# Hybrid decoder step on one core: GpSimd multiplies the prompt attention's probabilities by gate over sum

## The reference, cut to what matters

```
def masked_softmax(s, mask):
    m = jnp.max(jnp.where(mask, s, NEG_INF), axis=-1, keepdims=True)
    e = jnp.exp(jnp.where(mask, s - m, NEG_INF))
    return e / jnp.maximum(jnp.sum(e, axis=-1, keepdims=True), 1e-30)

o = g[:, :, 0] * o_c + g[:, :, 1] * o_s + g[:, :, 2] * o_w
```

## Time and profile before

| | before |
|---|---|
| median of three runs | 1538.82 us |
| the profiled execution, its own time | 1537.42 us |
| its span in the profile | 1535.6 us |
| PE busy | 94% |
| VectorE busy | 36% |
| ScalarE busy | 30% |
| GpSimd busy | 7% |
| the attention stage (871.2 to 1025.9 us) | 154.7 us |

### The profile page before, as it was taken

How to read it: one execution, slowest core, us unless ns; L and a number is a source line. 1 busy time by engine, 2 the same in 40 slices (tenths; PEclk the granted TensorE clock), 3 DMA queues, 4 the chain that set the end, 5 groups by cost and what they waited for, 6 DMA issues and landing times.

```text
span 1535.6 us, 28068 instructions
## 1 busy us (share of the span) xinstructions
PE 1438.0 (94%) x11334; PEld 1324.6 (86%) x11334; DVE 555.3 (36%) x1151; ACT 464.1 (30%) x751; POOL 112.9 (7%) x122
## 2 busy tenths in 40 slices
PE   7997999999999996999998989889789999999996
PEld 5676999999999996999998835459789999999995
DVE  0106323332323225335323274745443233232324
ACT  0115333332311114122212346643253333332111
POOL 0402000000001112000000000004320000000110
PEclk9998999999999997999999869989889999999998
DMA  9893444444433232232284323313212322323321
GB/s 347 291 369 110 139 162 137 163 137 161 133 92 87 84 103 54 86 93 69 83 97 157 126 81 102 99 50 116 83 56 82 95 83 86 92 65 87 86 84 67
DMA packets 83541, 180.21 MB, mean 117 GB/s; under 512 B 18341, under 2 KB 43429, under 8 KB 81742
## 3 DMA queue, kind: packets, MB, share of 16 engines
q1 hardware_dynamic: 83470, 179.23, 37.6%
HBM read 173.07 MB, written 10.28 MB: 119 GB/s over the span
## 4 chain that ended last, share of the span: by engine, by line
PE 86%; ACT 4%; DVE 4%; DMA 2%; SPq 2%; issue 2%; ACTq 0%; DVEq 0%
PE PS L1411 71%; PE PS L1334 4%; PE PS L1432 2%; DMA raw<-in_w_in 2%; PE PS L1603 1%; PE PS L1615 1%; SPq L574 1%; DVE rinv L937 1%; PE PS L1438 1%; PE PS L1315 1%; ACT uh L704 1%; PE PS L1348 1%; SPq L562 1%; PE PS L1628 1%; ACT sp L815 1%
## 5 line engine op out<-in xcount | busy, mean ns | idle before, releaser
L1411 PE MATMUL PS<-uh,wh 128*128 128x272 f32 x2032 | 428.8, 292 | 34.9 <-DVE ul L955 26.9
L930 DVE TENSOR_TENSOR wl<-raw,wh 128x1024 fp32r<-128x1024 f32 (+2 forms) x215 | 239.8, 1116 | 587.4 <-ACT wh L679 587.1
L679 ACT ACTIVATE wh<-raw 128x1024 fp32r<-128x1024 f32 (+2 forms) x215 | 203.6, 948 | 816.6 <-PE PS L1411 803.1
L1411 PE MATMUL PS<-uh,wl 128*128 128x272 f32 x2032 | 422.3, 290 | 0.0
L1411 PE MATMUL PS<-ul,wh 128*128 128x272 f32 x2032 | 421.7, 289 | 0.0
L1411 PEld LDWEIGHTS PS<-uh,wh 128*128 128x128 f32 x2032 | 320.5, 190 | 38.9 <-issue 36.1
L1411 PEld LDWEIGHTS PS<-ul,wh 128*128 128x128 f32 x2032 | 321.8, 190 | 0.0
L1411 PEld LDWEIGHTS PS<-uh,wl 128*128 128x128 f32 x2032 | 320.2, 190 | 0.0
L1411 PE MATMUL PS<-hh,wh 128*128 128x272 f32 x704 | 145.7, 288 | 0.9 <-DVE tmp L1004 0.9
L1411 PE MATMUL PS<-hh,wl 128*128 128x272 f32 x704 | 145.7, 288 | 0.0
L1411 PE MATMUL PS<-hl,wh 128*128 128x272 f32 x704 | 145.1, 288 | 0.0
(11 more groups left out here) (221 smaller groups left out, 1244.5 us busy)
## 6 DMA issues: line engine op xcount, KB each, us to landing
raw<-in_w_gu SPq DMA_DIRECT2D x88, 512.0 KB, 3.6
ada_t<-in_w_ada_t SPq DMA_DIRECT2D x44, 512.0 KB, 4.4
raw<-in_w_in SPq DMA_DIRECT2D x39, 512.0 KB, 3.6
ada<-in_w_ada SPq DMA_DIRECT2D x7, 2048.0 KB, 9.7
raw<-in_w_dn SPq DMA_DIRECT2D x32, 384.0 KB, 3.1
raw<-in_w_dn SPq DMA_DIRECT2D x32, 320.0 KB, 2.9
ch<-in_cmp_pages SPq DMA_DIRECT2D x64, 128.0 KB, 4.1
kv<-in_sel_pages SPq DMA_DIRECT2D x128, 64.0 KB, 1.9
```

The source lines that it names most:

```text
L679: e.activation(wh[:, u % SPLITS, 0:n, :], raw[:, u % RAWS, 0:n, :], ACT.Copy).then_inc(hi_ready, 1)
L930: e.tensor_tensor(wl[:, u % SPLITS, 0:n, :], raw[:, u % RAWS, 0:n, :], f(wh[:, u % SPLITS, 0:n, :]), ALU.subtract).then_inc(lo_ready, 1)
L1411: ins = mm(o[:, a, :], w[:, u % SPLITS, k, :], x[:, k0 + k, HT * a:HT * a + HT], start=(first and k == 0 and w is wh and x is xh), stop=(l ...
```

## The change

VectorE no longer multiplies the probabilities. After the factor is made it copies the four factors of the job from slot 5 to slot 0 of `stp` (the negative maximum there has been used by then) and raises a new semaphore, `p_factor`. GpSimd has a new function, `p_weights`, called for the 24 jobs in order between its part of the second norm and the addition of the mixers. It waits for the factor of the job and does the four multiplications in place. It raises the same semaphore, `p_prob`, on which the transposes wait as before.

```diff
+        p_factor = sem("p_factor")
...
+            def p_weights(j):
+
+                i, br, _ = JOBS[j]
+                n = nkeys(i, br)
+                e.wait_ge(p_factor, j + 1)
+                for r in range(GQ):
+                    e.tensor_scalar(sp[j % 3][:, r, 0:n], sp[j % 3][:, r, 0:n], stp[:, j % 3, 0, r:r + 1], None,
+                                    ALU.mult).then_inc(p_prob, 1)
+
             for n in range(4):
                 if n == 2:
+                    for j in range(len(JOBS)):
+                        p_weights(j)
                     for m in range(KD):
...
                 if br == 0 and i == 0:
                     chain(e.tensor_scalar(s[:, 5, :], s[:, 5, :], cst[:, C_VAL:C_VAL + 1], None, ALU.mult))
-                for r in range(GQ):
-                    e.tensor_scalar(sp[j % 3][:, r, 0:n], sp[j % 3][:, r, 0:n], s[:, 5, r:r + 1], None,
-                                    ALU.mult).then_inc(p_prob, 1)
+                e.tensor_copy(s[:, 0, :], s[:, 5, :]).then_inc(p_factor, 1)
```

## The result

The changed kernel takes 1578.78 us, median of four runs (1576.74 to 1580.95), against 1538.68 for the kernel before in the same comparison. The ratio is 1.0261, interval 1.0243 to 1.0279: 40 us slower (37 to 43). Forecast were 1551 us and a range to 1564, so the direction was right and the size was not. The profiled execution has a span of 1576.5 us, 40.9 more than before.

The account below looks back on a forecast made before the run. The order of work in the attention stage, not a full engine, was taken as the bound. Latency 7.7, contention 1.5 and clock 3.0 us make 12.2 on 1537.4: 1549.6, forecast 1551 against the median, range 1543 to 1564.

Parts of the forecast that it names:

- What bounds the kernel: Attention stage: no engine is full, the order of work bounds it; the multiplication's latency counts, VectorE mostly has time to spare.
- the price of GpSimd's multiplication: GpSimd's multiplication of one head: 0.24 us at 32 columns plus 1.0 ns a column, 0.72 us for 512 keys.
- bound from above: Upper limit for GpSimd's multiplication, from its sum of two tensors: 2.18 ns a column, 1.29 us for 512.
- the dear rival: GpSimd multiplies at line 618's price: latencies 18.0 us, with job 14, contention and clock 27, so 1566; chance 0.16.
- the sum's 12.2 us: Whole forecast loss: 7.7 us of added latency, 1.5 of GpSimd and VectorE delaying each other, 3.0 of lower PE clock.
- room: Time from the end of a job's fourth multiplication to when PE could use it; nearly 3 us in job 8.
- the ring: Last jobs: turn, copy, next job's exponentials, factor, multiplication, turn; jobs 21 to 23 add 3 x 1.02 us.
- looked the same: Jobs 2, 3, 5, 6, 9, 10, 12, 18, 20, like job 8: PE is behind, 1.4 us or more free.
- Job 17: Released VectorE starts its factor at once, 2.85 us late and not 3.65; with 1.26 this adds 0.46 us.
- Contention: GpSimd multiplying beside VectorE's sample chain (job 16) and scaling (job 17): 1.5 us, ends 0 and 1.85.
- The clock: New or longer PE stops at jobs 11, 15, 21: two stretches at the lower level, 3.0 us, ends 0 and 6.
- The faster rival: VectorE's line is the bound: release removes PE's 8.1 us of waits for adds, giving 1530.7; chance 0.06.

Follow-up runs that it names:

- assumed-price run: Changed kernel, but GpSimd multiplies only as many columns per head as cost the predicted price (182 of 512): ratio 1.0093, 14 us slower than the kernel before.
- the run that adds contention alone: Kernel before, VectorE's multiplications kept, plus GpSimd multiplications of a tile that nobody reads after each job: ratio 1.0007, 1 us.
- one column on VectorE: Kernel before, but VectorE multiplies only one column per head, the rest unscaled: ratio 0.9973, 4.2 us faster.
- exponentials first: Kernel before, but on ScalarE the next job's exponentials precede the copies of turned tiles also for two-tile jobs (18 to 23): ratio 0.9957, 6.6 us faster.

## Why the prediction was wrong

*What bounds the kernel* was right. The released time of VectorE buys next to nothing on the path: PE's waits for adds went from 8.1 to 7.4 us, and removing nearly all of the multiplication gives 4.2 us.

*The failed step is the price of GpSimd's multiplication*: "One tensor is read, so the memset is nearer." I ordered the costs by how many tensors are read, and wrote 0.72 us for 512 columns; the trace shows 1.56. The bound from above was a sum of two tensors, 2.18 ns a column, taken for dearer because it reads more. TENSOR_SCALAR takes 2.5 ns, so even the upper bound was too low, and the dear rival with it (27 us; measured 40). The 0.86 ns a column that the prediction gives as an estimate beside its sum is further off still. The assumed-price run shows that this was the error: at nearly the price I wrote, the sum's 12.2 us met a measured 14 (10 to 18).

At the measured price the same sum reads as follows. The fourth head is later by 0.27 + 6.19 - 1.68 = 4.8 us (512 keys), 3.8 (384), 2.75 (256) and 1.0 (few). The room to the fourth head was 3.7 us in jobs 8 to 10 and 1.8 in job 14, which makes 1.1 + 1.1 + 1.2 + 4.8 for block 3, 2.0 + 3.4 + 3.8 + 2.6 for block 2, 1.0 for job 19 and 3 x 2.75 in the ring: 29 us of 40. Jobs that "looked the same", with nearly 3 us free, were not free at this price.

*Job 17.* I had VectorE start at once, as it was the bound. With GpSimd's lateness the exponentials became the bound (3.73 us of wait), so the 0.8 us of release that I credited were not all there. The fourth head of job 17 added 4.0 us, and not the 2.6 that the sum above still grants it.

*Contention* was put too high: 1.5 us. GpSimd's four heads took 5.12 and 5.33 us in jobs 16 and 17 against 4.91 elsewhere, 0.6 us in all, and the run that adds contention alone gives 1 us. On the shared port pair (SBUF — State Buffer of the Trainium skill, Terms: held for the full instruction, the loser fully blocked) the trace agrees only that the two delay each other. The pass over two SBUF tensors began at 1000.70 us, 0.08 us after a GpSimd head of 1.24 us, and went from 1.09 to 1.44 us; blocked until that head's end, it would have taken some 2.2 (an estimate, as GpSimd's spans in a profile are rough). The sample steps mostly do not lie where it matters.

*The clock* was counted as two stretches, 3 us, and that was too little, too. PE has the same instructions in both kernels, so each can be held against its counterpart. Here are the scores behind job 11, the scores behind job 17, the sample products of job 20 and the first product with the output weights, before and then after:

```profile
953.47 1.56 PE L1603 MATMUL PS<-kT,qT 64*128 64x384 f32 x8
990.50 1.13 PE L1603 MATMUL PS<-kT,qT 64*128 64x256 f32 x8
1000.93 2.83 PE L1586 MATMUL PS<-kv,pT 128*32 128x128 f32 x96
1025.96 0.69 PE L1411 MATMUL PS<-oh,wh 128*128 128x272 f32 x2 [1.92 <-DVE ol L1257]
```
```profile
965.86 1.56 PE L1613 MATMUL PS<-kT,qT 64*128 64x384 f32 x8
1019.66 1.19 PE L1613 MATMUL PS<-kT,qT 64*128 64x256 f32 x8
1031.54 5.35 PE L1596 MATMUL PS<-kv,pT 128*32 128x128 f32 x96
1068.93 0.52 PE L1421 MATMUL PS<-oh,wh 128*128 128x272 f32 x2 [1.42 <-DVE ol L1267]
```

Behind the last head of job 11 PE works on without a wait up to the scores, 4.1 us before and 6.9 now. Behind job 17 it is 2.9 and 5.3, and the sample work of job 20 takes 3.7 and 6.8. In these three stretches the granted clock was 1.00 before and is 0.50 to 0.55 now. They cost 8.2 us: over each of them PE falls back by its part of that, and keeps this distance up to the next head that it waits for. Behind the stage 2.1 us go the other way: PE's first 3.6 us on the output weights ran at 0.53 before, and run at 1.00 now.

So the 41 us of the profiled executions are the 29 of latency by the sum, 8 of clock in three stretches, less 2 behind the stage. The other 6 lie in small pieces: 0.5 ahead of the stage, 0.6 in jobs 0 to 7, 0.3 in jobs 8 to 11, 2.6 in jobs 12 to 17 (1.4 of it the release granted to job 17) and 1.6 in the ring, where PE's part of a round runs at the lower clock. This is one execution of each kernel. In the profiles of two kernels that give GpSimd nothing here, the sample products took 4.81 us (one column on VectorE) and 4.57 us (exponentials first), so the 3 us of job 20 need not be due to the change.

*The faster rival* was excluded rightly: one column on VectorE gives 4 us, not 8.

## What to carry to other kernels

Before work is handed to another engine, ask for each instance how long its result lies unused, and compare that room with the added latency at the dearest price the operation may have; room that covers a cheap engine does not cover a slow one. An operation whose price no trace shows is not bounded by neighbours with more operands, so the bound from above needs a wide margin, or a few instructions timed in an idle stretch. And where a wait is a ring through several engines, look at the order in it first: here one condition on ScalarE gained 6.6 us, no less than the removal of nearly all of the multiplication, 4.2, as far as the intervals tell.

## What the runs showed of the hardware

- GpSimd in float32, per column of 128 partitions: copy 0.8 ns, TENSOR_TENSOR with one tensor twice or a broadcast column 1.7, TENSOR_SCALAR 2.5, pointer or immediate alike. With 512 columns: 0.61, 1.04, 1.56 us. One column still costs 0.29 us.
- VectorE's copy to the start of GpSimd's instruction: 0.27 us, of which 0.17 is the copy.
- PE's transposition of 128x128 went from 0.30 to 0.48 us from one head of job 11 to the next, behind stops of 0.62 and 1.15 us, and the granted clock from 0.98 to 0.50.
- The same work of PE behind job 11 took 4.1 us at a granted clock of 1.00 and 6.9 us at 0.55.
